# Sharing the work at the start, at two norms and at the last norm between engines and queues

## What is computed

```python
def first_block(x, ...):
    x = hybrid_layer(x, ...)     # rms_norm, x @ w_in, attention and recurrence, + merged @ w_out,
                                 # rms_norm, x @ w_peer_q, then experts u and v
    return rms_norm(x, norm_final_g)

def second_block(x, mem, ...):
    hn = rmsnorm(h, norm_mix_g); h = h + hybrid_mixer(hn, w_in, ...)
    hn = rmsnorm(h, norm_x_g)
    mn = rmsnorm(mem, norm_mem_g)
    h = h + cross_attention(hn, mn, w_xq, w_xkv, w_xo)
    hn = rmsnorm(h, norm_ffn_g)
    h = h + conv_glu(hn, w_up, conv_f_w, conv_f_b, w_down)
    return rmsnorm(h, final_g)
```

## Time and profile before

| what | us |
|---|---|
| runs | 1447.35, 1447.51, 1455.02 (median 1447.51) |
| the profiled execution's own time | 1447.28 |
| its span, first to last instruction | 1445.5 |
| PE busy | 1425.1 (99%) |
| DVE, ACT, POOL busy | 966.7, 734.4, 209.6 |

### The profile page before, as it was taken

How to read it: one execution, slowest core, us unless ns; L and a number is a source line. 1 busy time by engine, 2 the same in 40 slices (tenths; PEclk the granted TensorE clock), 3 DMA queues, 4 the chain that set the end, 5 groups by cost and what they waited for, 6 DMA issues and landing times.

```text
span 1445.5 us, 25160 instructions
## 1 busy us (share of the span) xinstructions
PE 1425.1 (99%) x10271; PEld 1290.1 (89%) x10271; DVE 966.7 (67%) x1746; ACT 734.4 (51%) x1055; POOL 209.6 (14%) x120
## 2 busy tenths in 40 slices
PE   8999999999999999999999999999999999999998
PEld 7989979999999999998777778888899888899986
DVE  5565674693944777778888876655577864677754
ACT  5673654545454444444444445544567754555543
POOL 5000000488883000000000000000014100000000
PEclk9999999999999999999999999999999999999999
DMA  6433446455555545555555566555443453455553
GB/s 237 145 131 102 162 161 210 140 179 186 180 186 178 172 162 172 165 163 173 175 164 172 168 223 240 186 184 185 160 152 122 152 180 108 158 178 187 187 184 111
DMA packets 66931, 245.07 MB, mean 170 GB/s; under 512 B 7424, under 2 KB 7552, under 8 KB 66560
## 3 DMA queue, kind: packets, MB, share of 16 engines
q1 hardware_dynamic: 66816, 243.45, 50.5%
HBM read 242.37 MB, written 1.05 MB: 168 GB/s over the span
## 4 chain that ended last, share of the span: by engine, by line
PE 93%; ACT 3%; DVE 2%; issue 1%; POOL 1%; DMA 0%; SPq 0%; DVEq 0%; POOLq 0%; ACTq 0%
PE bank L427 92%; ACT A L1038 1%; ACT whi L1038 1%; PE bank L436 1%; DVE wlo L1548 1%; ACT L1038 1%; DVE A L1548 0%; DVE A L1544 0%; DMA raw<-in_w_in_t 0%; POOL wlo L2347 0%; POOL small L2353 0%; DVE xres L1551 0%; DVE xres L1548 0%; ACT hTh L1038 0%; DVE hTl L1551 0%
## 5 line engine op out<-in xcount | busy, mean ns | idle before, releaser
L1548 DVE TENSOR_TENSOR wlo<-raw,whi 128x1024 fp32r<-128x1024 f32 x374 | 457.9, 1225 | 334.0 <-ACT whi L1038 333.5
L1038 ACT ACTIVATE whi<-raw 128x1024 fp32r<-128x1024 f32 x448 | 472.9, 1057 | 403.9 <-PE bank L427 402.5
L427 PE MATMUL bank<-hTh,whi 128*128 128x256 f32 x1944 | 555.2, 286 | 2.3 <-DVE wlo L1548 1.0
L427 PE MATMUL bank<-hTh,wlo 128*128 128x256 f32 x1944 | 548.8, 282 | 0.0
L427 PE MATMUL bank<-hTl,whi 128*128 128x256 f32 x1944 | 547.2, 281 | 0.0
L427 PEld LDWEIGHTS bank<-hTh,whi 128*128 128x128 f32 x1944 | 366.4, 188 | 6.9 <-DVE hTl L1551 2.5
L427 PEld LDWEIGHTS bank<-hTl,whi 128*128 128x128 f32 x1944 | 367.0, 189 | 0.3 <-issue 0.2
L427 PEld LDWEIGHTS bank<-hTh,wlo 128*128 128x128 f32 x1944 | 364.9, 188 | 0.0
L427 PE MATMUL bank<-whi,hTh 128*128 128x512 f32 (+2 forms) x552 | 218.3, 396 | 0.2
L2347 POOL TENSOR_TENSOR wlo<-raw,whi 128x1024 fp32r<-128x1024 f32 x74 | 177.3, 2398 | 274.9 <-ACT whi L1038 271.0
L427 PE MATMUL bank<-wlo,hTh 128*128 128x512 f32 (+2 forms) x552 | 215.0, 390 | 0.0
(11 more groups left out here) (171 smaller groups left out, 1373.4 us busy)
## 6 DMA issues: line engine op xcount, KB each, us to landing
raw<-in_u SPq DMA_DIRECT2D x128, 512.0 KB, 3.3
raw<-in_v SPq DMA_DIRECT2D x128, 512.0 KB, 3.3
raw<-in_w_up SPq DMA_DIRECT2D x44, 512.0 KB, 3.3
raw<-in_w_down SPq DMA_DIRECT2D x22, 512.0 KB, 3.3
raw<-in_w_in_t SPq DMA_DIRECT2D x18, 512.0 KB, 4.2
raw<-in_w_in_g SPq DMA_DIRECT2D x16, 512.0 KB, 3.3
raw<-in_w_out SPq DMA_DIRECT2D x16, 512.0 KB, 3.8
raw<-in_w_pq SPq DMA_DIRECT2D x16, 512.0 KB, 3.5
```

The lines of the kernel that those rows point to most:

```text
L427: return e.matmul(o, l, r, start=st, stop=sp_, skip_group_check=True)
L1038: return e.activation(o, i, func, **kw)
L1548: return e.tensor_tensor(o, a, b, op)
```

## The change

The pieces, in the order of the program:

1. **Start.** The second half of x is issued by ACT instead of SP; the constants come in two DMAs, unit 0 in two halves. Squares: ACT and DVE take one half of each row block each. The scaling of the first half of block 0 goes to ACT. The low parts of units 0 and 1 are halved between DVE and POOL. PE multiplies unit 0 tile by tile (`first_head`), then unit 1.
2. **Norms 1 and 5.** `lin_A` with `split` ends in two pieces of 256 columns, the very last in bank `bks[0]`. `part_add_and_sum` adds them one by one; the squares of the last 256 columns are DVE's. ACT scales block 0 (`scaled0`). `norm_head` takes units 0 and 1 together, tile by tile, and makes four of the transposes between matmuls.
3. **`bridge`.** ACT makes `whi` of unit `w_xk + 2` ahead of the squares; DVE makes both `rms_sum(4, ...)` ahead of the scaling.
4. **End.** POOL and DVE multiply by the last norm's weights into `xg` before the power is known, ACT scales with the power; one of the four output DMAs is ACT's.

```diff
 KEEP = [
-    ("ident", 128), ("iota", 128), ("iota16", 16),
-    ("g_mix", 8), ("g_ffn", 8), ("g_mix2", 8), ("g_x2", 8), ("g_mem2", 8), ("g_ffn2", 8),
+    ("ident", 128), ("g_mix", 8), ("g_ffn", 8), ("g_mix2", 8), ("g_x2", 8), ("g_mem2", 8), ("g_ffn2", 8),
+    ("iota", 128), ("iota16", 16),
...
 # PE
+            def norm_head(j, src, u0, spins):
+
+                for b in range(TB):
+                    if spins[b]:
+                        spin(spins[b], 7)
+                    for k in range(8 if b == 0 else 4):
+                        if b == 0 and k < 4:
+                            use(k)
+                        norm_tile(j, src, b, k)
+                bk = 4 + pair[0] % 3
+                use(bk)
+                wa, wb = (two(unit(u0 + i), KD) for i in range(2))
+                spin(spins[2], 7)
+                for k in range(KD):
+                    e.wait_ge(s["n_lo"], 8 * j + k + 1)
+                    if k < 4:
+                        norm_tile(j, src, 1, k + 4)
+                    h = [z[:, k, :] for z in hTv]
+                    ins = three(banks[bk][:, 0:256], [z[:, k, :] for z in wa], h, k == 0, k == KD - 1)
...
+                    ins = three(banks[bk][:, 256:512], [z[:, k, :] for z in wb], h, False, k == KD - 1)
...
-            norm_pe(1, scr, spins=(4, 2))
-            lin_T(BASE["w_pq"], 16, hTv, KD, normed(1, 4))
+            norm_head(1, scr, BASE["w_pq"], (4, 1, 2))
+            lin_T(BASE["w_pq"] + 2, 14, hTv, KD)
...
-            norm_pe(5, xs, spins=(4, 2))
-            lin_T(BASE["w_up"], 44, hTv, KD, normed(5, 4))
...
+            norm_head(5, xs, BASE["w_up"], (4, 1, 2))
+            lin_T(BASE["w_up"] + 2, 42, hTv, KD)
...
 # ACT
+            e.dma_start(xres[:, D:2 * D], x[P:2 * P, :]).then_inc(s_in2, 16)
             for b, landed in enumerate([s_in, s_in2]):
                 e.wait_ge(landed, 16)
-                for h in range(2):
-                    squares(xres, scr, b, h)
+                squares(xres, scr, b, 0)
+            scaled0(0, scr, 2)
...
             lin_A(BASE["w_out"], 8, hold=True)
-            residual_squares(0, scr)
+            part_squares(0, scr)
+            scaled0(1, scr)
             hi(BASE["w_pq"] + 1)
-            for k2 in range(4):
-                norm_hi(1, "g_ffn", hTv, k2)
+            norm_hi_tiles(1, "g_ffn")
...
             side.lists[0].append(bridge())
+            hi(BASE["w_xk"] + 2)
             side.step()
-            lin_T(BASE["w_xk"], 6, copy_to(kT2))
+            side.step()
+            hi(BASE["w_xk"] + 3)
+            e.wait_ge(s["w"], BASE["w_xk"] + 2)
...
 # DVE
+                e.wait_ge(s["acc2"], ACC2[stage])
+                tt(z, banks[b0 + 3][:, :], z, ALU.add).then_inc(s["r_part"], 1)
+                z = xres[:, D + 768:2 * D]
+                e.wait_ge(s["w"], last)
+                e.wait_ge(s["r_part"], PARTS[at])
+                tt(z, banks[b0][:, 0:256], z, ALU.add).then_inc(s["r_add"], 1)
+                e.wait_ge(s["r_add"], 4 * at + 4)
+                own(stt(scratch[:, D + 768:2 * D], z, 1.0 / D, z, ALU.mult, ALU.mult, accum_out=small[:, 8:9]))
...
+                own(ts(small[:, 9:10], st[:, 0:1], st[:, 1:2], EPS, ALU.add, ALU.add))
+                again()
+                tt(st[:, 3:4], small[:, 8:9], small[:, 9:10], ALU.add).then_inc(s["n_sum"], 1)
...
                 rms_sum(4, 0)
+                rms_sum(4, 1)
                 scaled(4, xres, scr3, 0)
-                rms_sum(4, 1)
...
 # POOL
             rstd(1)
-            e.wait_ge(s["n_scaled"], 16)
+            e.wait_ge(s["n_scaled"], 10)
             lo(BASE["w_pq"] + 1)
...
             rstd(6)
-            e.wait_ge(s["n_scaled"], 48)
+            e.wait_ge(s["n_scaled"], 38)
             lo(BASE["w_up"] + 1)
             units(BASE["w_up"], 66)
+            e.wait_ge(s_gf2, 16)
+            for h in range(2):
+                e.wait_ge(s["r_add"], 16 + h + 1)
+                c = slice(512 * h, 512 * h + 512)
+                e.tensor_tensor(xg[:, c], xres[:, c], gfin2[:, c], ALU.mult).then_inc(s["f_xg"], 1)
             rstd(7)
```

More of the change, by code:

```diff
@@ L139 @@
 ACC1 = {name: i + 1 for i, name in enumerate(("w_out", "v", "w2_out", "w_xo", "w_down"))}
+ACC2 = {name: i + 1 for i, name in enumerate(("w_out", "w_xo", "w_down"))}
+PARTS = {0: 1, 3: 2, 4: 3}
+SCALED = (0, 6, 10, 18, 26, 34)
+SCALED0 = {1: 2, 5: 6}
 B_TAPS = (2, 0, 0, 3, 6, 7, 7, 6)
@@ L1531, in act_program @@
                 ffn_rest(44 + u)
-            residual_squares(4, xs)
+            part_squares(4, xs)
+            for i in range(3):
+                if i == 0:
+                    e.wait_ge(s["n_rstd"], 15)
+                if i == 2:
+                    e.wait_ge(s["n_rstd"], 16)
+                    e.wait_ge(s["f_xd"], 1)
+                else:
+                    e.wait_ge(s["f_xg"], i + 1)
+                z = xg[:, i * 512:(i + 1) * 512]
+                act(z, z, ACT.Copy, scale=small[:, 4 * (i // 2) + 2:4 * (i // 2) + 3]).then_inc(s["f_act"], 1)
+            e.wait_ge(s["f_act"], 3)
+            e.dma_start(out[P:2 * P, 0:512], xg[:, D:D + 512]).then_inc(s_out, 16)
         def dve_program(e):
@@ L1592, in add_and_sum, with part_add_and_sum, part_norm, norm_lo_tiles @@
                 add(stage, b0, last, 1, 1)
+            def part_add_and_sum(stage, b0, last, r, scratch):
+                add(stage, b0, last, 0, 0)
+                add(stage, b0, last, 0, 1)
+                add(stage, b0, last, 1, 0)
+                rms_sum(r, 0)
+                at = {1: 0, 6: 3, 7: 4}[r]
+                z = xres[:, D + 512:2 * D]
+                e.wait_ge(s["acc2"], ACC2[stage])
[7 more added lines that the diff above has]
+                again()
+                st = small[:, 4:8]
+                e.wait_ge(s["n_sq"], 4 * r + 2)
+                own(ts(small[:, 9:10], st[:, 0:1], st[:, 1:2], EPS, ALU.add, ALU.add))
+                again()
+                tt(st[:, 3:4], small[:, 8:9], small[:, 9:10], ALU.add).then_inc(s["n_sum"], 1)
+            def part_norm(stage, b0, last, r, dst):
+                part_add_and_sum(stage, b0, last, r, dst)
+                scaled(r, xres, dst, 1)
+            def norm_lo_tiles(j, gname, tiles=range(KD)):
+                for k in tiles:
+                    e.wait_ge(s["n_hi"], 8 * j + k + 1)
+                    o = k // 4 * 256
+                    stt(hTv[1][:, k, :], banks[k % 4][:, o:o + 256], K_(gname, k, k + 1), hTv[0][:, k, :].bitcast(F32),
+                        ALU.mult, ALU.subtract).then_inc(s["n_lo"], 1)
             def residual_norm(stage, b0, last, r, dst):
```

247 lines of the change are left out of this document (183 added, 64 removed).

## The result

The changed kernel takes 1453.31 us (median of 20 executions, 1451.01 to 1461.94), the one before 1448.51 (20 executions on the same chips, 1447.08 to 1455.02). The ratio is 1.0036, with a 95% interval of 1.0024 to 1.0049: slower, by some 5 us, and outside the range that I gave. The profiled execution took 1452.79 us with a span of 1451.0 (before 1447.28 and 1445.5).

What follows compares the result with a forecast made beforehand. The prediction took TensorE, busy 1425.1 of 1445.5 us, as the bound. Its terms, -0.3 + 2.2 + 0.1 - 2.1 - 0.8 = -0.9, gave 1446.4 us profiled and 1446.6 median, range 1443.0 to 1451.5.

Steps and rivals of the forecast that it cites:

- narrow pieces: At three places, narrower last pieces cost 12 weight loads and matmuls instead of 6; counted as +0.1 us in all.
- Norms 1 and 5, +1.1 each: At both norms PE waits uncovered for POOL's low part, so the first pair ends later; +2.2 us together, bounds +0.6 to +3.2.
- The rival that the heads gain 1.0 each if POOL were out of the way: At norms 1 and 5, POOL done early enough makes each norm 1.0 us shorter, 1442.4 in all; chance 10%.
- The fall of the clock in that pause: At norms 1 and 5, PE's clock falls in the new pause, costing 2 us a norm; chance 28%.
- The start, -0.3: At the start, split squares and single-tile steps against a later x; -0.3 us, bounds -1.0 and +0.6.
- x late: At the start, if both halves of x share the transfer rate, the first lands at 5.6 instead of 4.33, costing 1.3 us.
- 0.63 for a square and 0.36 for the tiles: Start gains: squares on two engines save one 0.63 us square; single-tile steps leave 3 matmuls instead of 6, 0.36 us.
- isn't ready before 17.45: At the start, unit 2's readiness caps the gain: at most 0.65 us of an earlier first pair can be used.
- The bridge, -2.1: In the w_xk stage, the wait at unit 2 goes and the norm's powers come earlier; -2.1 us, bounds 0 and 2.8 gained.
- The rival that it gives nothing: At the bridge, PE meets at the transposes what it no longer waits at unit 2; 1448.7 us, chance 15%.
- The end, -0.8: In the tail, one DVE product follows the power instead of two, and the power comes slightly earlier; -0.8 us, bounds -1.3 and +0.3.
- my rival with two falls: PE's clock falls in the new pause at both norms, 2 us each: 1450.6 us; clock rival's chance 28%.

Runs made afterwards that it cites:

- out_on_sp: The changed kernel with the third of four output DMAs (block 1, columns 0 to 511) issued by SP instead of ACT; 1451.23 us, one execution.
- unit0_first: The changed kernel, but at norms 1 and 5 unit 0 alone goes tile by tile and POOL's low part is awaited behind its matmuls; 1445.49 us, ratio 0.9972.
- x_on_sp: The changed kernel with both halves of x issued by SP, one behind the other; 1452.96 us, ratio 1.0046.
- two_on_dve: The changed kernel without DVE's early product: DVE makes both block 1 products after POOL's power, ACT scales block 0, SP issues all outputs; 1458.72 us, one execution.
- lb_later: The changed kernel with the edits of x_on_sp and unit0_first, and unit 2's high and low part ahead of the start's small operations; 1442.16 us, one execution.
- zeros_ahead: The changed kernel with eleven products of zeros ahead of the wait for POOL at norms 1 and 5, instead of two behind it; 1447.78 us, ratio 1.0004.
- bridge_alone: The kernel before with only the bridge's two edits, early high part and both sums ahead of the scaling; 1445.96 us, ratio 0.9974.

## Why the prediction was wrong, step by step

The forecast was -0.9 us and the profiled executions differ by +5.5. Of the 6.4 between them 3.3 lie in the norms with their narrow pieces, 1.7 in the start, 1.3 in the mixers and 0.6 in the end; the bridge gave 0.6 more than forecast. Two terms lie outside the prediction's own bounds, the start (+1.42, bound +0.6) and the mixers' clock (put at nothing), and the norms' two falls fitted into the range only with every other term as forecast (1450.6). The medians differ by less, 4.8; why is said under the mixers below.

- **Norms 1 and 5, +1.1 each: right as a wait, wrong as a whole.** The wait was worked out well: POOL's low part begins 6.23 after the first add of w_xo (6.26 forecast) and ends at 8.58 (8.66), PE pauses for 2.54 (2.4), and where the clock doesn't fall the norm costs 1.24 (`out_on_sp`, norm 1) against the 1.1 forecast. The rival that the heads gain 1.0 each if POOL were out of the way was well priced too: 0.9 (`unit0_first`). The step that failed is the choice of case. The fall of the clock in that pause was a rival with 28%, priced at 2 us a norm. The runs put it at 1.6 a norm, and it is there in seven of the eight stretches with this pause that were profiled (two each in the changed kernel, `x_on_sp`, `out_on_sp` and `two_on_dve`). I had the evidence, the tail where the clock fell 2.0 us after PE's last work, and put too little on it. The Trainium skill (TensorE: Matmul & The Clock Gate, section What's actually happening) says that activity brings the full clock back; the windows above show it, 3.4 us after the fall.
- **The start, -0.3: +1.42.** x late was priced at 1.3 and measured at 1.31. The step that failed is what was set against it: the gains that the prediction works out, 0.63 for a square and 0.36 for the tiles, leave +0.3, and the -0.3 that it takes needs 1.6 of gains, for which it names no further term. `x_on_sp` shows 0.49 at the first pair. And the second pair loses 0.6 more, to the small operations ahead of unit 2 (`lb_later`). I had written that unit 2 "isn't ready before 17.45" and not asked how late it would be: PE got it at 19.23. The rule that several issuing engines are no separate queues (the Trainium skill, DMA: Bandwidth & Descriptors, section Issuing engines are not separate DMA queues) agrees with 4.9 and 5.1 us for halves that take 3.6 and 4.5 when issued in a row.
- **The bridge, -2.1: -2.7.** Mechanism right. The wait at unit 2 is gone, and the norm behind it starts its transposes 2.26 earlier. The term was too small by 0.6: the forecast stayed below its bound of 2.8, and POOL's power does take only 0.75 instead of 1.46, DVE's scaling 1.57 instead of 1.97. The rival that it gives nothing is out.
- **The end, -0.8: -0.17.** DVE's part was right: the power is blocked (0.94), the last result is there 0.87 earlier (0.8 forecast). The step that was missing is the transfers: I ended the sum at the last result and left the 2.4 behind it as it was. With two transfers issued together the span ends 3.17 after it. That the early product makes GpSimd's power wait is the rule of the Trainium skill (SBUF — State Buffer, section Who interferes with whom); `two_on_dve`, where the product is gone and the power takes 0.55, agrees.
- **Not in the prediction: the clock in the mixers, +1.3.** The profile of after has a fall at 1117 that before's lacks. Before's own executions lie in groups, 7 of 20 at 1447.1 to 1447.5, 9 from 1448.4 to 1449.1 and 4 at 1454.7 to 1455.0; after has 1 of 20 below 1452.5. With two norm falls and no other, after would take 1451.5 (1452.79 less 1.3), and only one of its executions is as low (1451.01; `out_on_sp`, with the mixers' fall but only one norm's, took 1451.23). So I read, from times and not from profiles, that it nearly always carries a fall in the mixers, and before in about two of three. This also moves the median that I started from: the three runs of before gave 1447.51, twenty give 1448.51. `unit0_first` has the mixers' fall without a fall at the norms, so it doesn't follow from those. Why it is more frequent after the change is open: no run here moves it by itself, and it needs no pause of PE.

The sum by what was measured: +1.42 + 2.80 - 2.66 + 1.26 + 2.84 - 0.17 = +5.49. Against my rival with two falls, 1450.6, the start is 1.7 more, the tail 0.6, the mixers 1.3, the bridge 0.6 less and the two norms 0.6 less: 1453.0, which is the profiled execution and the 0.2 by which I set the median above it.

## What to carry to other kernels

A wait that loses its cover is paid for (1.84 of 2.54 us here), and more if nothing keeps PE at work in it: put the fill ahead of the wait, where it costs nothing, not behind it. Before a piece of work is pulled forward, ask which operand of it comes last, and whether work that was in between had covered it. Time an output to its landing, and expect two transfers that become ready together to land later than two that become ready in turn (0.5 to 0.7 us here).

## What the runs showed of the hardware

- After a pause of 2.54 us PE's clock fell to half for 3.4 us of dense work at 7 of 8 places and not at the eighth; it fell between 0.19 us before PE started again (`out_on_sp`) and 0.65 after (`x_on_sp`). It cost 1.6 us. After before's waits of 0.79 us and 1.39 us it stayed at 1.00.
- Clock falls also come in dense stretches: 3.4 us long near 1117 (1.3 us lost), 3.4 or 13.65 us long near 136 (1.5 or some 6.2 lost). Five of the eleven profiles have one near 136 (`zeros_ahead` and `x_on_sp` a short one, `unit0_first`, `bridge_alone` and `two_on_dve` a long one). They are larger than most single edits here; most stretches of a profile can still be compared to 0.1 us when each is looked at for its clock.
- POOL's power of 128x1 took 0.55 us alone and 0.94 beside a DVE product with two inputs in SBUF.
- Two 512 KB loads issued at once from two engines' queues took 4.9 and 5.1 us, issued in a row from one 3.6 and 4.5.
